# Expert loop of a mixture layer: the remainder pass of every weight tile last, and one remainder subtraction moved behind the hidden state

## What is computed

```
def expert_block(args):
    xblk, e = args                                     # 128 rows of tokens
    gt = jnp.minimum(xblk @ w_gate[e] + b_gate[e], SWIGLU_LIMIT)
    up = jnp.clip(xblk @ w_up[e] + b_up[e], -SWIGLU_LIMIT, SWIGLU_LIMIT)
    hid = (up + 1.0) * (gt * jax.nn.sigmoid(SWIGLU_ALPHA * gt))
    return hid @ w_down[e] + b_down[e]
```

## Time and profile before

| what | value |
|---|---|
| runs | 1720.32 us median of 3 (1718.82 to 1720.41) |
| profiled execution | 1720.23 us |
| its span, first to last instruction | 1718.6 us |
| TensorE matmul busy | 1662.2 us (97%) |
| TensorE weight load busy | 1370.3 us (80%) |
| VectorE busy | 1436.0 us (84%) |
| ScalarE busy | 1266.6 us (74%) |
| granted TensorE clock, mean of the span | 0.995 |
| time from block to block in the loop | 35.98 us |

### The profile page before, as it was taken

One profiled execution on the slowest core, in us unless ns is written; L12 is line 12 of the kernel. 1 busy time (PEld: TensorE's weight loads), 2 busy tenths in 40 slices (PEclk: granted clock), 3 DMA queues, 4 the chain that ended last, 5 costly groups with the idle time before them and its releaser, 6 DMA issues.

```text
span 1718.6 us, 24492 instructions
## 1 busy us (share of the span) xinstructions
PE 1662.2 (97%) x8035; PEld 1370.3 (80%) x8035; DVE 1436.0 (84%) x1548; ACT 1266.6 (74%) x1452; POOL 501.1 (29%) x567
## 2 busy tenths in 40 slices
PE   9999898999899999999999999999999999999996
PEld 6777697788588888888888888888888888888885
DVE  5558877652459999999999999999999999999997
ACT  4553664562445888888888888888888888888884
POOL 4453741000025322323222222223222232322313
PEclk9999999999999999999999999999999999999998
DMA  7322000232207999999999999999999999999992
GB/s 256 123 95 84 18 1 26 98 115 82 110 13 311 377 383 360 373 361 385 380 369 369 360 380 383 373 359 369 374 382 379 355 376 368 380 378 355 379 345 98
DMA packets 53385, 476.19 MB, mean 277 GB/s; under 512 B 9991, under 2 KB 11144, under 8 KB 28770
## 3 DMA queue, kind: packets, MB, share of 16 engines
q1 hardware_dynamic: 42000, 450.69, 64.6%
q0 software_dynamic: 11152, 24.92, 6.4%
q10 hardware_dynamic: 194, 0.06, 0.0%
HBM read 461.24 MB, written 23.08 MB: 282 GB/s over the span
## 4 chain that ended last, share of the span: by engine, by line
PE 63%; DVE 17%; issue 13%; ACT 5%; POOL 1%; DVEq 0%; POOLq 0%; ACTq 0%
PE ps L1579 20%; PE ps L1537 18%; PE ps L1156 10%; DVE wsp L1927 6%; PE ps L1329 4%; PE ps L1564 2%; ACT extra L1053 2%; PE ps L1512 2%; DVE wf L1646 1%; DVE extra L2116 1%; DVE extra L2114 1%; DVE wsp_b L1927 1%; PE ps L1263 1%; PE ps L1251 1%; PE ps L1419 1%
## 5 line engine op out<-in xcount | busy, mean ns | idle before, releaser
L1927 DVE TENSOR_TENSOR wsp<-ring,wsp 128x1024 fp32r<-128x1024 f32 x512 | 600.6, 1219 | 32.2 <-ACT wsp L1008 32.1
L1008 ACT ACTIVATE wsp<-ring 128x1024 fp32r<-128x1024 f32 x388 | 386.5, 1052 | 69.0 <-PE ps L1523 53.4
L591 POOL TENSOR_TENSOR guard<-guard 1x1 f32<-1x1 f32 x190 | 128.5, 676 | 767.9 <-ACT extra L1076 309.1
L1537 PE MATMUL ps<-wsp,x_hi 128*128 128x512 f32 x1152 | 308.2, 389 | 0.6 <-DVE x_lo L2053 0.5
L1927 DVE TENSOR_TENSOR wsp_b<-ring,wsp_b 128x1024 fp32r<-128x1024 f32 x256 | 301.3, 1217 | 0.2 <-ACT wsp_b L1008 0.2
L1537 PEld LDWEIGHTS ps<-wsp,x_hi 128*128 128x128 f32 x1152 | 216.1, 188 | 46.2 <-issue 0.9
L1008 ACT ACTIVATE wsp_b<-ring 128x1024 fp32r<-128x1024 f32 x194 | 202.1, 1058 | 26.6 <-PE ps L1537 12.1
L1537 PE MATMUL ps<-wsp,x_lo 128*128 128x512 f32 x576 | 177.5, 389 | 0.0
L709 ACT ACTIVATE wf<-ring 128x1024 fp32r<-128x1024 f32 x80 | 84.4, 1056 | 114.7 <-PE ps L1156 59.6
L1646 DVE TENSOR_TENSOR wf<-ring,wf 128x1024 fp32r<-128x1024 f32 x64 | 84.5, 1325 | 98.7 <-ACT wf L709 98.7
L1156 PE MATMUL ps<-act_hi,wf 128*128 128x512 f32 x512 | 161.6, 397 | 2.5 <-DVE wf L1646 2.0
(11 more groups left out here) (388 smaller groups left out, 2945.4 us busy)
## 6 DMA issues: line engine op xcount, KB each, us to landing
ring<-in_w_gate_dram SPq DMA_DIRECT2D x32, 4096.0 KB, 15.1
ring<-in_w_up_dram SPq DMA_DIRECT2D x32, 4096.0 KB, 13.9
ring<-in_w_down_dram SPq DMA_DIRECT2D x32, 4096.0 KB, 13.1
ring<-in_w_in_dram SPq DMA_DIRECT2D x6, 2048.0 KB, 11.9
ring<-in_w_ckv_dram SPq DMA_DIRECT2D x4, 2048.0 KB, 10.8
ring<-in_w_out_dram SPq DMA_DIRECT2D x2, 2048.0 KB, 9.9
ring<-in_w_cq_dram SPq DMA_DIRECT2D x2, 2048.0 KB, 10.1
ring<-in_w_co_dram SPq DMA_DIRECT2D x2, 2048.0 KB, 9.9
```

The lines of the kernel that those rows point to most:

```text
L591: return pool.tensor_tensor(guard[:, i:i + 1], guard[:, 0:1], guard[:, 0:1], ALU.mult)
L1008: act.activation(split_w(c, 0), ring[:, m, k], ACT.Copy).then_inc(hi_ready, 1)
L1537: last = pe.matmul(ps[:, 2 * j + i], xp[:, k * P:(k + 1) * P], split_w(c, part)[:, i * 512:(i + 1) * 512], start=False, stop=(k == KT - 1 ...
L1927: dve.tensor_tensor(split_w(c, 1), ring[:, (GM + c // KT) % 3, c % KT], split_w(c, 0), ALU.subtract).then_inc(lo_ready, 1)
```

## The change

It does three things. In gate, the first five tiles of up, and down, the passes of a tile come in another order: rounded times rounded, remainder of the input times rounded weight, and last the rounded input times the weight's remainder. A tile's first pass waits for `hi_ready`, and only its last pass for `lo_ready`; the bias rows of up move behind that second wait. The last three tiles of up (`tile`, line 1523) keep the old order. And on VectorE the `lo` of tile 18, the third of down, stood ahead of `up` and `hid`; it now stands behind the second `hid` and ahead of the first `hid_lo`.

```
-                        pe.wait_ge(lo_ready, n * SPLIT + (c + 1))
-                        if c == UP_BIAS:
-                            bias_rows(1).then_inc(bias4_used, 1)
-                        for xp, part in ((x_hi, 0), (x_hi, 1), (x_lo, 0)):
+                        pe.wait_ge(hi_ready, n * SPLIT + (c + 1))
+                        for part, xp in enumerate((x_hi, x_lo, x_hi)):
+                            if part == 2:
+                                pe.wait_ge(lo_ready, n * SPLIT + (c + 1))
+                                if c == UP_BIAS:
+                                    bias_rows(1).then_inc(bias4_used, 1)
                             for i in range(2):
-                                last = pe.matmul(ps[:, 2 * j + i], xp[:, k * P:(k + 1) * P], split_w(c, part)[:, i * 512:(i + 1) * 512],
-                                                 start=False, stop=(k == KT - 1 and xp is x_lo))
+                                last = pe.matmul(ps[:, 2 * j + i], xp[:, k * P:(k + 1) * P], split_w(c, part // 2)[:, i * 512:(i + 1) * 512],
+                                                 start=False, stop=(k == KT - 1 and part == 2))
...
-                    pe.wait_ge(lo_ready, n * SPLIT + (c + 1))
+                    pe.wait_ge(hi_ready, n * SPLIT + (c + 1))
                     if k % HALF == 0:
                         pe.wait_ge(hidhi_ready, n * 2 + (k // HALF + 1))
-                    for xp, part in ((hid_hi, 0), (hid_hi, 1), (hid_lo, 0)):
-                        if xp is hid_lo and k % HALF == 0:
+                    for part, xp in enumerate((hid_hi, hid_lo, hid_hi)):
+                        if part == 1 and k % HALF == 0:
                             pe.wait_ge(hidlo_ready, n * 2 + (k // HALF + 1))
+                        if part == 2:
+                            pe.wait_ge(lo_ready, n * SPLIT + (c + 1))
...
-                for c in range(13, 19):
+                for c in range(13, 18):
                     lo(c, n * SPLIT + (c + 1))
...
                     dve.scalar_tensor_tensor(out=hid[:, hs], in0=gs[:, hs], scalar=CLIP, in1=up[:, hs], op0=ALU.min, op1=ALU.mult).then_inc(hid_ready, 1)
+                lo(18, n * SPLIT + 19)
                 for i in range(2):
                     dve.wait_ge(hidhi_ready, n * 2 + (i + 1))
```

More of the change, by code:

```diff
@@ L1571, in expert @@
                     c = GU + k
-                    pe.wait_ge(lo_ready, n * SPLIT + (c + 1))
+                    pe.wait_ge(hi_ready, n * SPLIT + (c + 1))
                     if k % HALF == 0:
                         pe.wait_ge(hidhi_ready, n * 2 + (k // HALF + 1))
-                    for xp, part in ((hid_hi, 0), (hid_hi, 1), (hid_lo, 0)):
-                        if xp is hid_lo and k % HALF == 0:
+                    for part, xp in enumerate((hid_hi, hid_lo, hid_hi)):
+                        if part == 1 and k % HALF == 0:
                             pe.wait_ge(hidlo_ready, n * 2 + (k // HALF + 1))
+                        if part == 2:
+                            pe.wait_ge(lo_ready, n * SPLIT + (c + 1))
                         for i in range(2):
-                            last = pe.matmul(ps[:, 4 + i], xp[:, k * P:(k + 1) * P], split_w(c, part)[:, i * 512:(i + 1) * 512],
-                                             start=(k == 0 and xp is hid_hi and part == 0), stop=(k == KT - 1 and xp is hid_lo))
-                            if k == KT - 1 and xp is hid_lo and i == 0:
+                            last = pe.matmul(ps[:, 4 + i], xp[:, k * P:(k + 1) * P], split_w(c, part // 2)[:, i * 512:(i + 1) * 512],
+                                             start=(k == 0 and part == 0), stop=(k == KT - 1 and part == 2))
+                            if k == KT - 1 and part == 2 and i == 0:
                                 last.then_inc(down_done, 1)
```

## The result

The changed kernel takes 1726.85 us (median of 6 runs, 1726.59 to 1728.87) against 1720.37 us (median of 6, 1718.82 to 1720.86): the ratio is 1.0042, with a 95% interval of 1.0029 to 1.0055. It is slower by some 0.4%, clear of the noise. The profiled execution has a span of 1725.0 us, 6.4 more than before.

A forecast was written before the change was run, and what follows sets the result against it. The prediction took TensorE's matmuls plus their holes to bound each loop block. From 1720.23 us, 31 x 0.29 - 1.0 = +8.0 gave 1728.2 us, with a range of 1722 to 1734.

The forecast's parts named there:

- The hole before the transposes: TensorE's wait for `hid` before the second-half transposes, each block: forecast to vanish, 0.49 us a block.
- The new order: Reordered passes in gate, up and down: `lo` needed 0.9 us later, worth nothing since TensorE did not wait for it.
- The second `up` waits for TensorE: VectorE, each block: the second `up` needs the last up matmul, so VectorE idles some 0.55 us.
- `hid_lo` reaches TensorE 3.63 after the start of the last up matmul: Down's first tile: `hid_lo` arrives at 1039.01, wanted at about 1038.4, a new hole of some 0.6 us.
- The restart: Down's first tile after the `hid_lo` wait: matmuls restart slowly, the tile's rest taking 1.05 us.
- A free restart: Down's first tile without slow matmuls after the wait: rest 0.91 us, a block gains only 0.15, +4.7 in all.
- 0.29 a block: Loop: the old hole of 0.49 is replaced by a costlier one, each block 0.29 us longer, about 36.27 us.
- The last block: Last block, bound by VectorE: second tile of down starts 1.2 us sooner; gain taken as 1.0, between 0 and 1.9.
- `hid_lo` did not come in time: Faster rival, down's first tile: `hid_lo` arrives before TensorE wants it, giving 1708.0 us; chance 0.07.
- The rival's price of 0.36 a block: Faster rival, second tile of down: starts 0.36 us sooner each block if `hid_lo` is in time; chance 0.07.
- The fall of the clock: Slower rival: a hole in down's first tile drops TensorE's clock each block, 1.7 us each, 1781 us; chance 0.03.
- nothing gives the loss back: Rest of each block: no later hole absorbs the 0.29 us; VectorE loses 0.07 of its 2.4 us to spare.

The follow-up runs named there:

- slow experiments: The changed kernel with tile 18's `lo` behind the first `hid_lo`, 1771.97 us; the same plus the old order in tiles 16 and 20, 1788.57 us.
- e3_hidlo_ahead: The changed kernel with the `lo` of tile 18 moved one place further back, behind the first `hid_lo`: 1771.97 us, ratio 1.0303.

## Why the prediction was right, step by step

**The hole before the transposes goes, and is worth 0.49.** Right: no idle time there in the loop. The run with the order alone kept it, and kept the time.

**The new order is worth nothing where TensorE did not wait for `lo`.** Right by the same run.

**The second `up` waits for TensorE.** Right: an idle time of some 0.55 was named, 0.58 was found, in each block.

**`hid_lo` reaches TensorE 3.63 after the start of the last up matmul** (1035.38 to 1039.01 in the working). In the profile after it is 1002.29 to 1005.92, the same 3.63. The sum of five VectorE rows and two latencies held to a hundredth, because each step had a row of the same kind.

**The restart.** The working had the second tile of down 1.05 after the weight load. In the profile it is 1006.50 plus the first tile's last two matmuls of 0.23 each, 1006.96, so 1.04 after 1005.92. A free restart, the lower end of the range, is out.

**0.29 a block.** From the first to the thirty-first hidden state, a block is 36.27 on average and was 35.98. Over 31 blocks that is some 9 us.

**The last block** was the term that was off: the forecast took 1.0 out of 0 to 1.9, and it gained 1.9, the upper end: 1.1 by its first transposes of the hidden state, ahead of which the idle time of 1.28 went, and 0.8 in down, where the clock did not fall. That this belongs to the change and was not luck is borne out by the other traces: from 2.9 to 6.3 us behind those transposes the clock was 0.51 and 0.63 in the two kernels with the `lo` of tile 18 ahead of `up` (before, and order alone), and 1.00 in the seven others. A further 0.5 of the 6.4 comes from ahead of the loop, where the first gate matmul started at 544.8 and not at 545.4; VectorE was as much ahead before it (a `lo` at 542.29 and not at 542.82), where nothing was changed. So 31 x 0.285 - 1.9 - 0.5 = 6.4, against the forecast's 8.0.

**The rivals.** `hid_lo` did not come in time. With the moved `lo` and the old order in two tiles it still came 0.27 late; with the `lo` in two halves on top it came in time. The halves with the new order in all tiles were not run. The rival's price of 0.36 a block for a kernel without the hole was near (0.26, by the block of 35.72). The remaining 0.1 lies in the step from ScalarE to TensorE: the working has down's first matmul 0.05 after the end of `hid_hi` (1037.88 to 1037.93), and in the kernel with the halves `hid_hi` ends at 999.65 and that matmul starts at 999.80, 0.15 later. The fall of the clock, as the result of a hole in each block, did not come with holes of 0.72; it came in the slow experiments, with holes such as that of 3.61. That nothing gives the loss back held here, but the reason that I gave (VectorE loses 0.07 of 2.4 us to spare) treats its idle time as one store of time. The two slow experiments show that one gap of 1.0 in it was in use by another engine.

## What to carry to other kernels

When a wait is taken away by moving an instruction back in a queue, follow the queue to the next instruction that cannot move with it: here one `up` that needs the last matmul stopped everything behind it, and the gain turned on whether the consumer wanted the result two or four matmuls later. Test the parts of a change alone and together: a free part and a good part made a loss. And before an engine's idle time is spent, ask who else runs in that gap: small GpSimd operations may need it, and the price shows up two engines further on, in a transfer that comes late.

## What the runs showed of the hardware that was not expected

A GpSimd operation on one element took 11.42 us while VectorE ran ten subtractions with two SBUF inputs back to back, and ended 0.04 us behind the last of them; with a gap made for it, it took 0.24 us. A hole of 3.61 us in TensorE's work was followed by a stretch of 3.4 us at a granted clock of 0.53, while a wait of 0.72 in each of 31 blocks left it at 1.00. The size of a hole alone did not settle it: in the same kernel (e3_hidlo_ahead) the hole of 3.28 that ended at 1438.93 was followed by a clock of 0.62 (1438.5 to 1443), and the hole of 3.29 that ended at 1328.05 by 1.00 (1327.5 to 1332).
